# Attention scores over the full 128 contraction rows, with each head's keys stored between zeroed rows

## What is computed

```python
HEAD_DIM = 64
# A: 8 query heads on 2 key heads        banded_attention(qa, ka, va, 127)
s = einsum('bhgnqd,bhnkd->bhgnqk', qp, kb) * HEAD_DIM ** -0.5
# B: 4 heads, two maps each              diff_attention
s1 = where(causal, einsum('bhqd,bhkd->bhqk', qb1, k1f) * scale, NEG_INF)
s2 = where(causal, einsum('bhqd,bhkd->bhqk', qb2, k2f) * scale, NEG_INF)
# C: 8 heads                             dilated_mixture
# I: 8 indexer heads on one key          dsa_attention
sc = relu(einsum('bhqd,bsd->bqhs', iqb, ikf) * IDX_DIM ** -0.5)
# D: 8 heads on one key
s = einsum('bhqd,bqkd->bhqk', qb, ksel) * HEAD_DIM ** -0.5
```

## Time and profile before

| | us |
|---|---|
| median of 3 runs | 3992.87 (3989.93 to 3992.98) |
| the profiled execution | 3993.01 |
| its span, first to last instruction | 3991.2 |
| TensorE matmuls busy | 3932.5 (99%) |
| VectorE busy | 2644.5 (66%) |
| ScalarE busy | 1987.7 (50%) |
| GpSimd busy | 507.7 (13%) |

### The profile page before, as it was taken

How to read it: one execution, slowest core, us unless ns; L and a number is a source line. 1 busy time by engine, 2 the same in 40 slices (tenths; PEclk the granted TensorE clock), 3 DMA queues, 4 the chain that set the end, 5 groups by cost and what they waited for, 6 DMA issues and landing times. The chain is left out here.

```text
span 3991.2 us, 63940 instructions
## 1 busy us (share of the span) xinstructions
PE 3932.5 (99%) x20356; PEld 3326.4 (83%) x20356; DVE 2644.5 (66%) x5020; ACT 1987.7 (50%) x2846; POOL 507.7 (13%) x716
## 2 busy tenths in 40 slices
PE   8999999999999999999999999999999999999997
PEld 7778888888888888888777788888888888888886
DVE  6655678658865555555676556886588655555556
ACT  4554544654565444444455545456545654444443
POOL 1000000640072000000010000007301720000000
PEclk9999999999999999999999999999999999999999
DMA  6435556559645666666554354564596456666665
GB/s 221 144 120 203 177 187 208 173 188 292 215 169 189 241 232 229 226 232 228 212 173 142 124 204 175 194 204 175 194 282 212 176 203 229 230 230 225 231 230 207
DMA packets 244353, 810.89 MB, mean 203 GB/s; under 512 B 24976, under 2 KB 157584, under 8 KB 158864
## 3 DMA queue, kind: packets, MB, share of 16 engines
q1 hardware_dynamic: 207376, 775.84, 56.0%
q10 hardware_dynamic: 36864, 33.57, 2.4%
HBM read 756.89 MB, written 52.43 MB: 203 GB/s over the span
## 5 line engine op out<-in xcount | busy, mean ns | idle before, releaser
L1047 DVE TENSOR_TENSOR lo<-raw,hi 128x1024 fp32r<-128x1024 f32 x1312 | 1617.9, 1233 | 1010.3 <-ACT hi L724 979.5
L724 ACT ACTIVATE hi<-raw 128x1024 fp32r<-128x1024 f32 x1312 | 1388.5, 1059 | 1509.6 <-PE bank L678 756.8
L460 PE MATMUL bank<-xhl,hi 128*128 128x512 f32 x4608 | 1631.4, 398 | 1.8 <-ACT scr L879 1.4
L461 PE MATMUL bank<-xhl,lo 128*128 128x256 f32 x4608 | 1290.1, 280 | 0.0
L460 PEld LDWEIGHTS bank<-xhl,hi 128*128 128x128 f32 x4608 | 866.1, 188 | 202.0 <-ACT scr L879 1.8
L461 PEld LDWEIGHTS bank<-xhl,lo 128*128 128x128 f32 x4608 | 870.8, 189 | 0.0
L676 PE MATMUL bank<-hi,xhl 128*128 128x512 f32 x2048 | 797.9, 390 | 3.0 <-DVE gelu_out L1341 2.6
L678 PE MATMUL bank<-hi,xhl 128*128 128x512 f32 x2048 | 797.5, 389 | 0.0
L677 PE MATMUL bank<-lo,xhl 128*128 128x512 f32 x2048 | 797.5, 389 | 0.0
L676 PEld LDWEIGHTS bank<-hi,xhl 128*128 128x128 f32 x2048 | 384.5, 188 | 83.9 <-DVE gelu_out L1341 3.3
L678 PEld LDWEIGHTS bank<-hi,xhl 128*128 128x128 f32 x2048 | 384.5, 188 | 79.7
(11 more groups left out here) (143 smaller groups left out, 2438.3 us busy)
## 6 DMA issues: line engine op xcount, KB each, us to landing
raw<-u_t SPq DMA_DIRECT2D x256, 1024.0 KB, 5.0
raw<-v_t SPq DMA_DIRECT2D x256, 1024.0 KB, 4.8
raw<-w_in SPq DMA_DIRECT2D x84, 1024.0 KB, 4.8
raw<-w_out SPq DMA_DIRECT2D x32, 1024.0 KB, 4.7
raw<-wq SPq DMA_DIRECT2D x32, 1024.0 KB, 4.8
gelu_scratch<-gelu_out ACTq DMA_DIRECT2D x256, 128.0 KB, 3.9
scr<-gelu_scratch SPq DMA_DIRECT2D x256, 128.0 KB, 4.6
gates_scratch<-arena SPq DMA_DIRECT2D x32, 512.0 KB, 9.9
```

Source lines behind the costliest of these rows:

```text
L460: pe.matmul(acc[:], wh, xhl[:, c, :, :].rearrange("p a t -> p (a t)"), start=(c == 0), stop=False)
L461: return pe.matmul(acc[:, L:2 * L], wl, xh[:, c, :], start=False, stop=(c == DC - 1))
L724: act.activation(hi[j % NSPLIT][:], half, ACT.Copy).then_inc(hi_done, 1)
L1047: dve.tensor_tensor(lo[j % NSPLIT][:], half, hi[j % NSPLIT][:].bitcast(F32), ALU.subtract).then_inc(lo_done, 1)
```

## The change

The contraction of a score matmul now runs over all 128 rows. The query operand is the whole pair, that is two heads. The key operand is a pair that holds the wanted key in its 64 rows and zeros in the other 64, so the second head adds nothing. Each key pair therefore needs two homes: one with the upper key and zeros below, and one with the lower key and zeros above. The new homes take the room of pairs that are not yet or no longer in use, and `ln2_gb` moves from pairs 16 to 31 to pairs 4 to 19.

GpSimd writes the zeros (`pad`, seven memsets in each layer), and a new semaphore `padded` is waited for by every score item. ScalarE stores the three key groups in two or three instructions of 64 rows instead of one of 128.

```diff
-PAIR = {"ak": 0, "dk": 2, "ik": 3, "iq": 4, "aq": 8, "dq": 12, "bq": 16, "bk": 20, "cq": 24, "ck": 28}
+QUERY_PAIR = {"I": 4, "A": 8, "D": 12, "B": 16, "C": 24}
+UPPER_HOME = {G_MIX: 0, G_BK: 20, G_CK: 28}
+LOWER_HOME = {G_MIX: ((28, 4),), G_BK: ((0, 2), (10, 2)), G_CK: ((16, 4),)}
...
 def score_operands(kind, h, part):
...
+    q = QUERY_PAIR[kind] + (h if kind == "B" else h // 2)
+    lower = part if kind == "B" else h % 2
+    group = {"B": G_BK, "C": G_CK}.get(kind, G_MIX)
+    k = {"I": 3, "A": h // 4, "D": 2, "B": h, "C": h // 2}[kind]
+    if not lower:
+        return q, UPPER_HOME[group] + k
+    return q, [base + i for base, n in LOWER_HOME[group] for i in range(n)][k]
+
+PADS_FOR = {"I": 3, "A": 3, "D": 3, "B": 5, "C": 7}
...
-        ln2_gb, _ = region(16 * L, 2, D)
+        ln2_gb, _ = region(4 * L, 2, D)
...
                     def scores(n):
-                        qp, kp, half = score_operands(kind, h, part)
-                        rows = slice(HD * half, HD * half + HD)
+                        qp, kp = score_operands(kind, h, part)
+                        pe.wait_ge(padded, PADS_FOR[kind])
...
-                            last = pe.matmul(bank[4 + n % 2][:, block_cols[b]], qk_t[rows, qp, b * P:(b + 1) * P],
-                                             qk_t[rows, kp, 0:(b + 1) * P], start=True, stop=True)
+                            last = pe.matmul(bank[4 + n % 2][:, block_cols[b]], qk_t[:, qp, b * P:(b + 1) * P],
+                                             qk_t[:, kp, 0:(b + 1) * P], start=True, stop=True)
...
                     def store_rope(r, b):
-                        act.activation(qk_t[:, 4 * r:4 * r + 4, b * P:(b + 1) * P],
-                                       bank[6][:].rearrange("p (a b) -> p a b", a=4), ACT.Copy).then_inc(staged_read, 1)
+                        if r not in UPPER_HOME:
+                            act.activation(qk_t[:, 4 * r:4 * r + 4, block], src, ACT.Copy).then_inc(staged_read, 1)
+                            return
+                        at = UPPER_HOME[r]
+                        act.activation(qk_t[0:HD, at:at + 4, block], src[0:HD], ACT.Copy)
+                        done = 0
+                        for at, n in LOWER_HOME[r]:
+                            last = act.activation(qk_t[HD:P, at:at + n, block], src[HD:P, done:done + n, :], ACT.Copy)
+                            done += n
+                        last.then_inc(staged_read, 1)
...
+                    def pad(rows, at, n):
+                        pool.memset(qk_t[rows, at:at + n, :], 0.0).then_inc(padded, 1)
+                        pads[0] += 1
+                        pool.wait_ge(padded, pads[0])
+
+                    upper, lower = slice(0, HD), slice(HD, P)
+                    pad(lower, UPPER_HOME[G_MIX], 4)
+                    pad(upper, *LOWER_HOME[G_MIX][0])
+                    pad(lower, UPPER_HOME[G_BK], 4)
                     for r in range(N_ROPED):
+                        if r == G_BK:
+                            pool.wait_ge(scored, ITEM_NO["A", 7, 0] + 1)
+                            for at, n in LOWER_HOME[G_BK]:
+                                pad(upper, at, n)
...
+                    pool.wait_ge(scored, ITEM_NO["B", 3, 1] + 1)
+                    pad(upper, *LOWER_HOME[G_CK][0])
+                    pool.wait_ge(scored, ITEM_NO["D", 7, 0] + 1)
+                    pad(lower, UPPER_HOME[G_CK], 4)
```

More of the change, by code:

```diff
@@ L266, in build @@
         staged, staged_read = sem("staged"), sem("staged_read")
-        irelu, iacc = sem("irelu"), sem("iacc")
+        irelu, iacc, padded = sem("irelu"), sem("iacc"), sem("padded")
         scored, masked_done = sem("scored"), sem("masked_done")
@@ L752, in store_rope @@
                         act.wait_ge(staged, TURN_NO["rope", r, b] + 1)
-                        act.activation(qk_t[:, 4 * r:4 * r + 4, b * P:(b + 1) * P],
-                                       bank[6][:].rearrange("p (a b) -> p a b", a=4), ACT.Copy).then_inc(staged_read, 1)
+                        block = slice(b * P, (b + 1) * P)
+                        src = bank[6][:].rearrange("p (a b) -> p a b", a=4)
+                        if r not in UPPER_HOME:
[8 more added lines that the diff above has]
+                        last.then_inc(staged_read, 1)
                     def store_probs(kind, h):
@@ L983, in _ @@
                 def _(pool):
+                    pads = [0]
+                    def pad(rows, at, n):
[6 more added lines that the diff above has]
+                    pad(lower, UPPER_HOME[G_BK], 4)
                     for r in range(N_ROPED):
+                        if r == G_BK:
+                            pool.wait_ge(scored, ITEM_NO["A", 7, 0] + 1)
+                            for at, n in LOWER_HOME[G_BK]:
+                                pad(upper, at, n)
                         for b in range(NB):
```

## The result

The changed kernel takes 3961.24 us (median of 4 runs, 3959.75 to 3962.91), the kernel before 3992.57 us (4 runs). The ratio is 0.9923, with a 95% interval of 0.9906 to 0.994. The prediction was 3964 us, 3959 to 3970. The profiled execution took 3962.91 us, its span is 3961.1 us.

A forecast was written before the change was run, and what follows sets the result against it. TensorE's stream was taken as the bound. The profiled 3993.01 us less 29.3 for the score items plus 0.4 for layer starts gave 3964.1, the median 0.14 lower: predicted 3964 us, range 3959 to 3970.

The forecast's parts named there:

- What bounds the kernel: Attention stage: TensorE's stream is the bound, so a us taken out of it is a us of the total.
- The price of an item: Score item on TensorE: 0.66 us over 128 rows instead of 1.06, 0.99 or 1.04; 29.3 us saved.
- What was added: ScalarE stores, GpSimd memsets, TensorE waits and VectorE load in the stage: cost 0; layer starts 0.2 us each.
- The tightest place: Bank 6, between the last group's store and the next write: 1.4 us of room shrink to 0.8, cost 0.
- The cover of the two memsets ahead of `G_BK`: GpSimd queue before the adds of `G_BK`: some 7 us of slots against 0.9 us of memsets, cost 0.
- the starts of the layers: Three first memsets delay VectorE's first split, for which TensorE waits: 0.2 us a layer, between 0 and 1.
- the rival of GpSimd against VectorE: Memsets hold up VectorE's splits of two SBUF inputs; 5.4 us lost at layer starts, 3970 us; chance 0.03.
- The granted clock: Layer starts and normalizations: half-clock stretches may come out longer or shorter, 3.5 us both ways over four places.

The follow-up runs named there:

- the kernel with the matmul part alone: Kernel before with only its score matmuls reading all 128 rows; no zeroed rows, memsets, split stores or new wait: 3961.47 us, ratio 0.9924.
- the kernel with pairs over full rows: Changed kernel (128 rows, zeroed homes) with the two heads of a pair scored by turns in one slot: 3965.38 us, ratio 0.9928.

## Why the prediction was right

**What bounds the kernel.** Right. Each of the stages shortened by what its items lost, and the stages behind them kept their length: from the end of the stage to the start of the last matmul of the output projection it is 105.33 us after and 105.37 before (284.69 to 390.02, 299.44 to 404.81).

**The price of an item.** Right in its terms. Alone 1.11 us (forecast 1.11), with transposes of probabilities 1.44 (1.46), with value products 2.07 (2.07). A 128-row item costs 0.64 to 0.66 us, where the sum had 0.66. 256-column float32 records, for which no row of 128 partitions existed, run at 0.22 us each: twice the 128-column one. By the spans the 80 items lose 22 × 0.39 + 32 × 0.34 + 26 × 0.39 = 29.6 us; by the stages it is 2 × 15.03 = 30.1, and 30.2 with the two entries that this measure leaves out. The small rest lies in the ten or so matmuls behind each item.

**What was added.** Right: all at zero. The memsets are 0.95 and 0.52 us long, near the 0.9 and 0.45 taken from the 2048-column one. ScalarE's stores of 64 rows last 0.59 us, as long as those of 128. The tightest place was bank 6 at the last rotary group: its store ends at 248.77 and the next transposes start at 249.44, 0.67 us later, where I had 0.8. The profile of ScalarE there:

```profile
247.57 0.59 ACT L760 ACTIVATE arena<-bank 64x512 f32<-64x512 f32 x1
248.18 0.59 ACT L763 ACTIVATE arena<-bank 64x512 f32<-64x512 f32 x1
```

The cover of the two memsets ahead of `G_BK`, some 7 us by the forecast, was the 6.18 us shown above.

I had put 0.4 us on the starts of the layers. From the first matmul to the last one ahead of the first score item, layer 1 takes 67.10 us in the changed kernel and 67.02 in the kernel before. Its three memsets run from 11.41 to 14.36, and VectorE's first split starts behind them, at 14.54, so this start says nothing on the rival of GpSimd against VectorE. A later place does. VectorE's two splits around the memsets at 242.82 in the changed kernel:

```profile
242.82 1.96 POOL L999 MEMSET arena<- 64x1024 f32 x2
```

```profile
241.98 1.98 DVE L1078 TENSOR_TENSOR lo<-raw,hi 128x1024 fp32r<-128x1024 f32 x1
...
244.14 1.21 DVE L1078 TENSOR_TENSOR lo<-raw,hi 128x1024 fp32r<-128x1024 f32 x1
```

And the same two splits in the kernel with the matmul part alone, which has no memsets:

```profile
240.44 1.98 DVE L1047 TENSOR_TENSOR lo<-raw,hi 128x1024 fp32r<-128x1024 f32 x1
...
242.61 1.21 DVE L1047 TENSOR_TENSOR lo<-raw,hi 128x1024 fp32r<-128x1024 f32 x1
```

The lengths are the same with and without memsets beside them. The first split is long in both kernels: an add of GpSimd, 1.29 us long, started ahead of it and runs beside it. So the loss that the rival feared exists for the adds, which both kernels have, and not for the memsets.

**The granted clock.** The swing I allowed for is there. Stretches of 40 us around the start of layer 2, in the kernel before and in the changed one (length, busy us of PE, PEld, DVE, ACT, POOL, granted clock, DMA share, GB/s):

```profile
1985.00:2025.00 40.00, 27.52 (x135) 24.24 (x134) 31.29 (x52) 26.97 (x40) 0.00 (x0) 0.83 0.41 130
```

```profile
1970.00:2010.00 40.00, 27.69 (x129) 24.35 (x128) 30.66 (x51) 26.63 (x40) 2.84 (x3) 0.79 0.40 129
```

The clock is 0.79 of full where it was 0.83. From the first matmul of layer 2 on, the start (to the last matmul ahead of the first score item) cost about 1.2 us more, the normalization of layer 1 cost 1.6 more, that of layer 2 1.1 less, and what lies behind the two, the expert passes above all, was 1.8 less. Together with the 30.2 from the stages that makes the 30.4 us between the two traces from the first matmul to the last (the spans differ by 30.1). These swings differ from one execution to the next of one kernel, with the memsets and without. In the second trace of the changed kernel the start of layer 2 takes 64.82 us and not 65.49, and the normalization of layer 1 takes 14.95 and not 16.56. The kernel with the matmul part alone, without memsets, and the kernel with pairs over full rows, with memsets, both take 64.15 for that start.

The medians differ by 31.3 us, where 28.9 were forecast: 0.8 from the items (30.1 for 29.3), 0.4 that the layer starts didn't cost, and 1.2 on top. That last part is within what the same kernels vary between two measurements: the changed kernel gave 3961.24 and 3964.73 us, 31.3 and 28.3 us below the kernel before. So the mechanism was right and the price of the items right to 1 us; how near the median came to the point beyond that is chance.

## What to carry to other kernels

Look at starts, not at busy time: 99% busy hid 30 us of gaps of 0.1 to 0.3 us. Where a few matmuls with half the contraction rows stand in a stream of full ones, each entry and each exit cost about 0.2 us here, and reading zeros in the other half cost less than switching. It is better still to gather the half-row matmuls and to give both halves work: two heads then take the time of one, the switch is paid once, and no zeros are needed.

## What the runs showed of the hardware

- A change between 64 and 128 contraction rows cost about 0.2 us each way for float32 weights of 128 columns: 0.1 us in which no load starts, and 0.1 us of a load in the open. It cost the same inside an item as at its edges: an item alone spans 1.50 us in both. With transposes behind the item the pair of changes at the edges cost 0.34 us instead of 0.39, the one inside still 0.39; that is the stage of 221.68 us against 220.87.
- 64-row matmuls in different row halves ran fully at the same time, 1.06 us for two heads instead of 1.71 in the same half (1.57 against 0.93 us for eight records).
- The overlap didn't depend on the order in which the two heads were written: 1.51 us in both. Written one behind the other, the second head's 128-key matmuls started ahead of the first head's 256-key ones (four records of 128 keys before any of 256). The Trainium skill says otherwise, "TensorE: Matmul & The Clock Gate", What overlaps and what doesn't: matmuls start and end in program order. The measurement decides here for the starts, for different row halves and different banks; the ends are modelled in the trace and tell nothing.
- VectorE's splits (two SBUF inputs) and GpSimd's adds of 512 columns slow each other. In the changed kernel they overlap twelve times between 60 and 330 us, and the one that started first keeps its length (add 1.29 us, split 1.21) while the other is longer: 1.68 to 2.00 us for eight splits, 2.19 to 2.33 for four adds. Beside a memset of GpSimd (0.6 us of overlap) a split kept its 1.21 us.
- Whether two halves could write one PSUM bank at the same time was not tried; each head had its own.
